# One hybrid diffusion trunk step: three of four convolution tiles on TensorE, both probability halves scaled on VectorE

## The reference

```python
def depthwise_conv(x, w, b):
    y = lax.conv_general_dilated(
        x, w[:, None, :], window_strides=(1,), padding=[(CONV_K // 2, CONV_K // 2)],
        dimension_numbers=('NWC', 'WIO', 'NWC'), feature_group_count=x.shape[-1])
    return y + b
...
    def one_block(qblk):
        s = jnp.einsum('bqkgd,bskd->bkgqs', qblk, k).astype(jnp.float32) * scale
        p = jax.nn.softmax(s, axis=-1).astype(v.dtype)
        return jnp.einsum('bkgqs,bskd->bqkgd', p, v)
...
    glu = a[..., :CONV_CH] * jax.nn.sigmoid(a[..., CONV_CH:])
    conv = jax.nn.silu(layer_norm(depthwise_conv(glu, conv_w, conv_b), cn_g, cn_b))
    return jnp.concatenate([attn, conv], axis=-1) @ w_out, own_kv
```

## Time and profile before

| | us |
|---|---|
| median of 3 runs | 1388.37 (1386.95 to 1389.29) |
| the profiled execution | 1388.3 |
| its span, first to last instruction | 1386.4 |
| first score matmul of the attention stage | at 380.31 |
| first matmul of the output projection | at 422.37 |

### The profile page before, as it was taken

One profiled execution on the slowest core, in us unless ns is written; L12 is line 12 of the kernel. 1 busy time (PEld: TensorE's weight loads), 2 busy tenths in 40 slices (PEclk: granted clock), 3 DMA queues, 4 the chain that ended last, 5 costly groups with the idle time before them and its releaser, 6 DMA issues.

```text
span 1386.4 us, 21119 instructions
## 1 busy us (share of the span) xinstructions
PE 1369.1 (99%) x8065; PEld 1331.8 (96%) x8065; DVE 972.0 (70%) x1474; ACT 552.5 (40%) x758; POOL 47.8 (3%) x50
## 2 busy tenths in 40 slices
PE   7999999999999999999999999999999999999999
PEld 6999999999948999999999999999998999999999
DVE  5698889948885988888338888888385688443522
ACT  4433333235476643333227433332275463333320
POOL 0000000011001200000002000000020100000000
PEclk8999999999999999999999999999999999999999
DMA  9766567533411465664334665664334253333331
GB/s 377 302 226 229 223 224 246 201 136 120 136 57 62 167 231 220 229 226 168 121 125 177 222 230 226 229 232 166 128 115 164 97 211 135 134 121 136 137 125 73
DMA packets 48758, 245.65 MB, mean 177 GB/s; under 512 B 6336, under 2 KB 10688, under 8 KB 28096
## 3 DMA queue, kind: packets, MB, share of 16 engines
q1 hardware_dynamic: 48416, 244.80, 48.4%
q10 hardware_dynamic: 288, 0.13, 0.0%
HBM read 240.80 MB, written 1.70 MB: 175 GB/s over the span
## 4 chain that ended last, share of the span: by engine, by line
PE 95%; DVE 2%; DMA 1%; ACT 1%; SPq 0%; issue 0%; DVEq 0%; ACTq 0%
PE ps L1419 30%; PE ps L1421 30%; PE ps L1420 30%; DMA m_raw<-in_w_pairs 1%; PE ps L1825 1%; PE ps L1826 1%; PE ps L1827 1%; PE ps L1480 0%; DVE conv L1182 0%; PE ps L1754 0%; PE ps L1496 0%; PE ps L1716 0%; PE ps L1728 0%; DVE smax L1253 0%; PE ps L1854 0%
## 5 line engine op out<-in xcount | busy, mean ns | idle before, releaser
L1419 PE MATMUL ps<-a_hi,w_hi 128*128 128x384 f32 x1552 | 522.4, 337 | 1.5 <-DVE a_lo L1394 1.2
L1420 PE MATMUL ps<-a_lo,w_hi 128*128 128x384 f32 x1552 | 519.3, 335 | 0.0
L1421 PE MATMUL ps<-a_hi,w_lo 128*128 128x384 f32 x1552 | 519.3, 335 | 0.0
L904 DVE TENSOR_TENSOR w_lo<-w_raw,w_hi 128x2048 fp32r<-128x2048 f32 x153 | 352.0, 2302 | 179.6 <-ACT w_hi L594 179.6
L594 ACT ACTIVATE w_hi<-w_raw 128x2048 fp32r<-128x2048 f32 x153 | 291.8, 1910 | 245.6 <-DMA w_raw<-in_w_units 245.5
L1419 PEld LDWEIGHTS ps<-a_hi,w_hi 128*128 128x128 f32 x1552 | 291.8, 188 | 8.0 <-issue 3.4
L926 DVE SCALAR_TENSOR_TENSOR m_raw<-m_raw 128x1024 f32<-128x1024 f32 x256 | 299.2, 1219 | 0.0
L1420 PEld LDWEIGHTS ps<-a_lo,w_hi 128*128 128x128 f32 x1552 | 292.0, 188 | 0.1
L1421 PEld LDWEIGHTS ps<-a_hi,w_lo 128*128 128x128 f32 x1552 | 291.9, 188 | 0.0
L1421 PE MATMUL ps<-h_hi,w_lo 128*128 (+1 forms) x704 | 235.1, 334 | 0.0
L1419 PE MATMUL ps<-h_hi,w_hi 128*128 (+1 forms) x704 | 235.1, 334 | 0.0
(11 more groups left out here) (198 smaller groups left out, 863.6 us busy)
## 6 DMA issues: line engine op xcount, KB each, us to landing
w_raw<-in_w_units SPq DMA_DIRECT2D x153, 1024.0 KB, 4.8
m_raw<-in_w_rows SPq DMA_DIRECT2D x128, 512.0 KB, 5.5
m_raw<-in_w_pairs SPq DMA_DIRECT2D x5, 1024.0 KB, 14.0
p_raw<-in_w_pairs SPq DMA_DIRECT2D x3, 1024.0 KB, 24.5
m_raw<-padded SPq DMA_DIRECT2D x32, 53.4 KB, 2.4
x<-in_x_cols SPq DMA_DIRECT2D x2, 768.0 KB, 5.5
out<-x SPq DMA_DIRECT2D x8, 192.0 KB, 1.9
m_raw<-in_c_ctx SPq DMA_DIRECT2D x1, 512.0 KB, 8.0
```

The costliest lines, as they stand in the source:

```text
L904: nc.vector.tensor_tensor(w_lo[:, slot(u), :], w_raw[:, slot(u), :], w_hi[:, slot(u), :].bitcast(FP32), ALU.subtract).then_inc(lo_done, 1)
L1419: mm(out, whi, mhi, start=start, stop=False)
L1420: mm(out, whi, mlo, start=False, stop=False)
L1421: return mm(out, wlo, mhi, start=False, stop=stop)
```

## The change

Convolution tile 2 moves from VectorE's taps to TensorE's quads, so that tiles 1, 2 and 3 are made there and tile 0 alone by taps (`DVE_TILES` 2 to 1). The quads grow from 16 to 24, and their places and those of the evictions are new: six before the loop, two in steps 0, 2, 3, 4, 5, 7, 8, 9 and 10, and evictions in steps 0, 5 and 10. The third tile has its own stationary weights (`quad_w2`) and takes ring slot 4 of `m_raw` for its shifted copies; the DMAs of the three tiles stand behind the loads of units 8, 9 and 10. The scaling of the first half moves from ScalarE to VectorE, ahead of that of the second half. VectorE takes the maximum of step m + 2 in step m, from step 0 on, where it took that of m + 1 from step 1 on. The sum of the convolution tiles is spread: each evicted tile is added in the step after its eviction.

```diff
--- before.py
+++ after.py
@@ -48,7 +48,7 @@
 MODT = N_MOD * KT
 RMS_EPS, LN_EPS = 1e-6, 1e-5
 COND_GROUP = 32
-DVE_TILES = 2
+DVE_TILES = 1
 QUADS = 8
 GROUPS = 4
 PAD_W = PAD_N + 1
@@ -247,6 +247,7 @@
         smaxn = sb("smaxn", [P, HEADS * TT], stack=r)
         ssum = sb("ssum", [P, HEADS * TT], stack=r)
         srec = sb("srec", [P, HEADS * TT], stack=r)
+        quad_w2 = sb("quad_w2", [P, GROUPS * QUADS, COND_GROUP], stack=r)
         r.close()
         r = ExitStack()
         o_g = sb("o_g", [P, 2, CONV_CH], stack=r)
@@ -377,9 +378,11 @@
             return m_raw[:, 1, 0:(QT + 1) * LAT].rearrange("p (j t) -> p j t", t=LAT)
 
         def quad_x(i):
-            return m_raw[:, i, 0:GROUPS * QUAD_N].rearrange("p (g n) -> p g n", g=GROUPS)
+            return m_raw[:, (0, 1, 4)[i], 0:GROUPS * QUAD_N].rearrange("p (g n) -> p g n", g=GROUPS)
 
         def quad_w(i):
+            if i == 2:
+                return quad_w2[:]
             return m_raw[:, 2, i * UNIT // 2:(i + 1) * UNIT // 2].rearrange("p (q c) -> p q c", c=COND_GROUP)
 
         def even_part(g, n):
@@ -560,7 +563,7 @@
                                         quad_wt[:, i].rearrange("p g q -> p (g q)").unsqueeze(2)
                                         .to_broadcast([P, GROUPS * QUADS, COND_GROUP]), ALU.mult).then_inc(quad_ready, 1)
 
-            pool.wait_ge(quad_ready, 2)
+            pool.wait_ge(quad_ready, CT - DVE_TILES)
 
             def add_channel_squares(m, sq):
 
@@ -805,9 +808,6 @@
                     mix_high((m - 4) // TT)
                 if m:
                     flipped_copy(m - 1)
-                act.wait_ge(rec_done, m + 1)
-                nc.scalar.activation(probs(m)[:, 0, 0:width(m)], probs(m)[:, 0, 0:width(m)], ACT.Copy,
-                                     scale=srec[:, 2 * m:2 * m + 1]).then_inc(prob_done, 1)
                 if m in QUAD_OUT:
                     quad_evict(QUAD_OUT.index(m))
             flipped_copy(PAIR_STEPS - 1)
@@ -1259,42 +1259,40 @@
                 dve.wait_ge(exp_done, m + 1)
                 nc.vector.reciprocal(srec[:, 2 * m:2 * m + 2], ssum[:, 2 * m:2 * m + 2]).then_inc(rec_done, 1)
 
-            def scale_second(m):
+            def scale(m):
                 width = CTX if m % TT == 0 else LAT + PAST
                 dve.wait_ge(rec_done, m + 1)
-                nc.vector.tensor_scalar(probs(m)[:, 1, 0:width], probs(m)[:, 1, 0:width], srec[:, 2 * m + 1:2 * m + 2], None,
-                                        ALU.mult).then_inc(half_scaled, 1)
+                for h, done in ((0, prob_done), (1, half_scaled)):
+                    nc.vector.tensor_scalar(probs(m)[:, h, 0:width], probs(m)[:, h, 0:width],
+                                            srec[:, 2 * m + h:2 * m + h + 1], None, ALU.mult).then_inc(done, 1)
 
             def mix_low(j, src):
                 dve.wait_ge(mix_hi, j + 1)
                 nc.vector.tensor_tensor(a_lo[:, j, :], src, a_hi[:, j, :].bitcast(FP32), ALU.subtract).then_inc(mix_ready, 1)
 
             split(u + 8)
-            dve.wait_ge(glu_done, 3)
-            taps(2, 0, 7)
             glu_mul(3)
             attention(0)
             attention(1)
             dve.wait_ge(glu_done, CT)
+            dve.wait_ge(conv_done, DVE_TILES)
             for m in range(PAIR_STEPS):
                 reciprocals(m)
-                scale_second(m)
+                scale(m)
                 if m >= 4 and (m - 4) % TT == 0:
                     mix_low((m - 4) // TT, ps[:, 0, 0:TOK])
-                if 1 <= m < PAIR_STEPS - 1:
-                    attention(m + 1)
-                k = 7 + 2 * m + min(m, 3)
-                taps(2, min(k, CONV_K), min(k + 2 + (m < 3), CONV_K))
-                if m == PAIR_STEPS - 2:
-                    dve.wait_ge(conv_done, DVE_TILES)
-                    a = mark(nc.vector.tensor_tensor(conv_sum(), conv[:, 0, :], conv[:, 2, :], ALU.add))
-                    dve.wait_ge(dve_self, a)
-                    dve.wait_ge(quad_out, 1)
-                    a = mark(nc.vector.tensor_tensor(conv_sum(), conv_sum(), conv[:, 1, :], ALU.add))
-
-            dve.wait_ge(dve_self, a)
-            dve.wait_ge(quad_out, 2)
-            nc.vector.tensor_tensor(conv_sum(), conv_sum(), conv[:, 3, :], ALU.add).then_inc(conv_summed, 1)
+                if m + 2 < PAIR_STEPS:
+                    attention(m + 2)
+                if m - 1 in QUAD_OUT:
+                    i = QUAD_OUT.index(m - 1)
+                    dve.wait_ge(quad_out, i + 1)
+                    if i:
+                        dve.wait_ge(dve_self, a)
+                    ins = nc.vector.tensor_tensor(conv_sum(), conv_sum() if i else conv[:, 0, :], conv[:, QUAD_TILES[i], :], ALU.add)
+                    if i < len(QUAD_OUT) - 1:
+                        a = mark(ins)
+                    else:
+                        ins.then_inc(conv_summed, 1)
             mix_low(QT - 1, ps[:, 0, 0:TOK])
 
             def layer_norm(m, src, dst, sq, at):
@@ -1894,9 +1892,9 @@
 IDLE_BANK, BUSY_SUMS, BUSY_SPREAD = 1, 2, 6
 SCORE_BANK = [4, 2]
 PAIR_STEPS = QT * TT
-QUADS_AT = [4, 1, 1, 1, 1, 0, 2, 1, 1, 1, 1, 1, 1]
-QUAD_OUT = [4, 11]
-QUAD_TILES, QUAD_LOAD = [1, 3], [8, 10]
+QUADS_AT = [6, 2, 0, 2, 2, 2, 2, 0, 2, 2, 2, 2, 0]
+QUAD_OUT = [0, 5, 10]
+QUAD_TILES, QUAD_LOAD = [1, 2, 3], [8, 9, 10]
 
 SUM_BANK = [6, 4]
 BC_BANK = [(5, 5), (4, 5)]
```

## The result

The changed kernel takes 1392.3 us, the median of 7 runs (1390.03 to 1395.19), beside 1386.95 for the kernel before in the same comparison (7 runs, 1385.67 to 1389.29). The ratio is 1.0038, 95% interval 1.0029 to 1.0047: 5.3 us slower, between 4.0 and 6.5. Forecast were 1392.2 us, a loss of 3.9, and "slower" with a chance of 0.75. The sign came out as forecast; the loss is 1.4 us larger than the stage's sum. That the time itself was met within 0.1 us is luck: the forecast added 3.9 to 1388.37, the median of three runs, and the four later runs of the kernel before took the median of all seven down by 1.4, just as much as the loss was larger.

A forecast was written before the change was run, and what follows sets the result against it. TensorE, busy 99% of the span, was taken to bound the kernel. Quads +5.1, opening eviction +1.7, middle waits -3.4 and last eviction +0.5 gave +3.9 us on 1388.3, so 1392.2; range 1389.6 to 1395.0.

The forecast's parts named there:

- Quads, +5.1: TensorE in the attention stage: 24 quads in 10 bursts take 17.5 us, where 16 in 12 took 12.4.
- the fit: Price of a burst of n quads on TensorE, from bursts of one, two and four: 0.14 + 0.67 n us.
- The upper price of 0.78 a quad: Upper bound on TensorE: eight more quads at the mean price of 0.78 would cost 6.2 us.
- Eviction at step 0, +1.7: Stage opening: the eviction waits for eight quads and holds exponentials 1, so scores 3 wait; +1.7 us, bounds 1.2 to 2.0.
- Eviction at step 10, +0.5: Stage end: the eviction on ScalarE lengthens the wait before values 10 from 1.2 to 1.7 us; bounds 0 and 0.9.
- Middle, -3.4: Middle steps of the stage: TensorE's 3.6 us of waits shrink to 0.2; bounds 0 or 1.2 left.
- Costs at nothing: Third weight build, 16 more DMAs and spread convolution sums, around and in the stage: hidden, no cost.
- The third build: GpSimd's third stationary-weight build: delays VectorE about 1.9 us, 1.1 passes on towards the keys, a slack of 1.3 hides it.
- The transfers: SyncE's queue: tile 2's copies land before 390.5, its first quad comes at 392.4, a reserve of 2 us.
- The sum: Whole stage: 5.1 + 1.7 - 3.4 + 0.5 = +3.9 us, stage end near 426.3, time 1392.2 us.

The follow-up runs named there:

- the second: The changed kernel measured again with no edit, against the kernel before: 1391.9 us, median of 5, ratio 1.0035.
- The kernel without waits over 0.7: The changed kernel with evictions in steps 1, 5 and 11 in place of 0, 5 and 10: stage 43.98 us, ratio 1.0015 against the kernel before.
- the respaced one: The kernel before with the maximum two steps ahead and taps, quads and first eviction at other places: 1383.77 us, ratio 0.9975.

## Why the prediction came out right

*Quads, +5.1.* Right. Bursts of 4.16 for six and 1.48 for two are the fit to the hundredth; 24 quads took 17.5 us. The upper price of 0.78 a quad is excluded. The drain that the Trainium skill names for a changed tiling mode (TensorEngine Tiling (Array Packing), Key Properties) is in line with it: the fixed 0.14 stayed when the burst was six long. No run here leaves the change of mode out, so that the drain is its cause is not shown.

*Eviction at step 0, +1.7.* Right, shown by the move of that eviction: 1.65 of idle time went and 0.54 came in its place.

*Eviction at step 10, +0.5.* Right in the change (1.61 idle where there was 1.13). As a cause it is larger: the move by one step left 0.69, so the eviction is worth 0.9, and the other parts of the change took 0.4 from the old wait.

*Middle, -3.4.* Right in size: no marked wait is left there. The prediction named the lighter VectorE and the earlier maximum in one breath and didn't say whether either would do. The experiments show that both are needed: without the taps but with the late maximum 4.0 us of waits are back, and with the earlier maximum but the taps in their old places the stage stays at 42.06. What the lighter VectorE gives, new places for taps, quads and the first eviction give too (39.14).

*Costs at nothing.* The third build delayed VectorE. The first tap took 2.08 us in place of 0.48, while GpSimd's build, 3.97 where the one ahead of it took 1.92, was waiting in its turn for VectorE's split:

```profile
328.45 3.95 DVE L904 TENSOR_TENSOR w_lo<-w_raw,w_hi 128x2048 fp32r<-128x2048 f32 x1
332.33 2.08 DVE L1178 TENSOR_SCALAR conv<-padded,conv_wt,vec_b 128x399 f32<-128x399 f32 x1
...
368.66 0.55 DVE L1245 TENSOR_TENSOR qk<-qk,ps 128x384 f32<-128x384 f32 x1
...
330.21 3.97 POOL L561 TENSOR_TENSOR quad_w<-mod_pick,quad_wt 128x1024 f32<-128x1024 f32 x1
```

Against the start of the stage the keys came 0.7 us later than in the earlier trace rows (1.1 were expected), and nothing waited for them. The transfers fit as well: tile 2's went out from 376.27 for 10.0 us, and its first quad ran at 391.65 without a wait.

```profile
376.27 10.01 SPq L507 DMA_DIRECT2D m_raw<-padded  x16
...
386.96 11.11 SPq L507 DMA_DIRECT2D m_raw<-padded  x16
```

*The sum.* +3.9 forecast, +3.91 in the trace. What the medians show beyond it, 1.4 us in the first comparison and 1.0 in the second, had no term in the prediction. A part may be the sample: the profiled execution of before, 1388.3 us, is itself 1.3 above the median of its seven runs, and the two profiled executions of the changed kernel, 1391.56 and 1392.25, are 3.3 and 4.0 above that.

The list of spans and clocks on record narrows the rest down, though no run was made for it. First, the time of an execution exceeds its span by 1.8 us (1.7 to 1.9) in the kernel before and by 2.15 (2.1 to 2.2) in the changed one: 0.3 us lie outside the span. The kernel with the first half on ScalarE, run once, is back at 1.8; why is not known. Second, the executions of the changed kernel have a lower mean clock more often: 0.994 or less in 6 of 12, against 9 of 44 of the kernel before. Among executions of the same mean clock the spans differ by about the stage's 3.9:

| mean clock | before, mean span (runs) | changed, mean span (runs) | difference |
|---|---|---|---|
| 0.996 | 1384.8 (10) | 1388.6 (2) | 3.8 |
| 0.995 | 1385.8 (25) | 1389.4 (4) | 3.6 |
| 0.994 | 1386.6 (9) | 1390.7 (5) | 4.1 |

These are few executions, and the clock stands there in thousandths, each worth about 1 us. Still, the rest beyond the sum goes with the clock. Where in the execution it was low these numbers don't say: all fourteen traces, those of the two kernels too, have stretches of half clock outside the stage, 7 to 17 us at the start and, in all but one, a short one near 312. Three traces show that the clock can fall to half within this stage and cost 1.6 to 2.7 us there, but the changed kernel's own two traces are at full clock in it, and filling one of its two long waits changed nothing that can be measured. Whether the other, before values 10, is the place in the unprofiled executions was not tried. The kernel without waits over 0.7 has a ratio of 1.0015 for a stage of +1.9, 0.2 us beyond it, which the 0.3 outside the span cover; the respaced one has 0.9975 for -2.9. That speaks for long waits as the condition, and does not show it: the place of this last 1 us stays open.

## What to carry to other kernels

Price a move between engines by the engine that sets the end: here 20 us of VectorE's work went away (31 taps), and the stage grew by what TensorE took on, less waits that a better order would have removed anyway. An eviction that waits for a long accumulation belongs in an in-order queue behind the work that feeds the critical engine: one place further down was worth about 1 us each time (1.1 and 0.9). Where three engines hand work round a loop, look one step ahead and at the spacing together; each alone gave 0.3 us at most, both gave 2.9 without moving any work.

## What the runs showed of the hardware

Within this stage the granted clock fell from full to half in three of fourteen traces, none of them of the two kernels themselves. Twice TensorE had just ended a wait, 0.5 us earlier in the one (1.65 long) and 0.2 in the other (1.61); in the third the clock fell 0.7 us into a wait of 1.83. It came back after 3.4 to 6.9 us, in which TensorE was busy but for the rest of that third wait and one of 0.58. Thirteen other waits of 1.5 to 1.7 us, in these and the other traces, passed without it. So the same wait can cost 1.6 us or twice that.

VectorE's tensor-scalar (one tensor read) was held up while GpSimd built weights, 2.08 us for a tap of 0.48, and so was a tensor-tensor (3.95 for 2.29). The Trainium skill, SBUF — State Buffer, "SBUF: two separate sides", describes the port pair of the two as an exclusive lock that is taken for a whole instruction, on VectorE's side by one with two inputs in SBUF or in a mode that uses both ports; no row shows the mode of the tap. The rows agree otherwise, since the two engines' instructions end one behind the other (GpSimd's second build at 330.2, the split at 332.4, the third build at 334.2, the tap at 334.4) and the split, the third build and the tap are each longer by about what was left of the other engine's instruction.
